# Interleaving two weight pieces by token tile, and moving one tile's norm from VectorE to ScalarE and GpSimd

## The chip, the core and the metric

The kernel runs on one NeuronCore of a Trainium2 chip. The metric is the device time of one execution in microseconds (us). The engines are TensorE (PE), VectorE (DVE), ScalarE (ACT), GpSimd (POOL) and SyncE (SP, which here only starts transfers). Each works through its own instruction stream in order and waits on semaphores for the others. All arithmetic is fp32; a product of two fp32 matrices is made of three matmuls on a high part (rounded to fp32r) and a low part (the rest) of each operand.

## The reference, cut to what matters

One decoder layer over 512 tokens of width 1024: a mixer of three attention-like parts, then cross attention into 256 memory tokens, then a mixture of experts, each with an RMS norm ahead and a residual add behind, and a final norm. The change lies between the second and the third:

```python
x = x + memory_cross_attention(rms_norm(x, xattn_norm_g), rms_norm(mem, mem_norm_g), wq, wk, wv, wo)
                                # its last step is  o @ wo,  512x1024 by 1024x1024
h = rms_norm(x, ffn_norm_g)     # x * rsqrt(mean(x*x) + EPS) * g, per token
coarse, fine = h @ w_coarse + b_coarse, h @ w_fine + b_fine     # 4 + 16 router logits a token
# group by argmax, top 2 of its 4 experts, then SwiGLU experts on the chosen tokens
```

## The kernel before, in words

The 512 tokens lie as four tiles of 128 (`NT` = 4), tile t in `X[:, t, :]`. Weights come in pieces of 128 x 2048 floats. For each piece SP loads it into one of three `raw` buffers, ACT copies it to a high part `whi`, DVE subtracts to a low part `wlo`, and PE multiplies. `whi` and `wlo` have two slots each (`SPLIT` = 2), so piece n is split only when piece n-2 has been multiplied to its end (`wait_consumed`).

The output projection `wo` of the cross attention is the last four pieces, `xo0` to `xo3` (`ND` is their end, so `xo2` is `ND - 2` and `xo3` is `ND - 1`). `xo0` and `xo1` are the upper and lower half of the contraction for output columns 0 to 511, `xo2` and `xo3` those for columns 512 to 1023. Each piece has four groups, one a token tile, of 12 matmuls 128x128 by 128x512. The groups of `xo2` and of `xo3` for a tile add into the same PSUM bank; DVE then adds the bank to X (the eviction, L1249). PE takes the pieces whole: all four tiles of `xo2`, then all four of `xo3`.

When a tile's last group is evicted, several engines work on that tile. Call this the tile's tail:

- ACT squares X with a row sum (`square_last`, L797); POOL makes the factor 1/rms from it (`rms`, L650 and L653, count `rms_done`); DVE writes h = X * factor * gain to `H3` in an interleaved column order (`norm_last`, L1165, count `h_done`). SP stores X to `xod` and H3 to `h3d`.
- PE transposes the unnormed X (`norm_transposes`, eight transposes to two banks, L1753); ACT copies them to `ahi` (`norm_hi`, L804), DVE subtracts to `alo` (`norm_lo`, L1172). The factor of a token is applied to its logits later, and the gain is already in the router weights.

Then PE multiplies the router weights with the tokens of tiles 0 and 1 into `ps[0]`, and with those of tiles 2 and 3 into `ps[1]` (`narrow`, 16 matmuls each, L1767 and L1769, count `route_mm`). ACT copies each out (`router_out`, L1025, to `rT`), PE turns them to token rows in `ps[2]` (`to_tokens`, L1774), and DVE starts a long chain of small instructions at L1467 that ends in the lists of tokens of each expert. Off that chain hang one-hot ranks on PE (L1944, L1948), the gather of the first expert's tokens by matmuls from H3 (L1956, which waits for `h_done`), the weight splits of the first expert's pieces (L791 on ACT, L1153 on DVE), and then the loop over the experts, six pieces a turn. After its splits ACT waits for `h_done` of all tiles, starts a transfer of the final gain, and makes two exponentials that DVE asks for at L1511.

In the kernel before, the transposes of tile 0 stand between the last two groups of `xo3`, those of tiles 1 to 3 after them. DVE runs `norm_last` of tiles 2 and 3 last, just ahead of L1467. SP asks for the expert pieces 6 to 9 only after `h_done` of all tiles.

Of the kernel before, what the change touches and what calls it, by code (L numbers as in the profile page):

```python
# [79 lines left out]
def build(nc, A, C, out):  # L80

    O = offsets()
    with ExitStack() as ctx:
# [3 lines left out]
        def sem(name):  # L87
            return ctx.enter_context(nc.semaphore(name))
# [196 lines left out]
            quarter(f"xo{b}", wo, b, NT, "dve")  # L285
        ND = len(pieces)
        NMP = ND + 4
        ORDER = sorted(KEY, key=KEY.get)
        of_piece = [[g for g, x in enumerate(groups) if x[0] == n] for n in range(ND)]

# [2 lines left out]
        sums = 0  # L293
        for g, x in enumerate(groups):
            if x[1] == "H" and x[3] == 1:
                tiles = len(of_piece[x[0]])
                bank_of.append(bank_of[g - tiles])
                before_bank.append(None)
            else:
                bank_of.append(sums % DRING)  # L300
                before_bank.append(last_on.get(sums % DRING))
                sums += 1
            if x[5]:
                last_on[bank_of[g]] = g
# [25 lines left out]
            return s2_hi[:, :], s2_lo[:, :]  # L330


        LATE_SPLITS = (KEY["win"], ND - 2, ND - 1)

        def evacs(g, eng):
# [94 lines left out]
        cum_mm = sem("cum_mm")  # L430
        cum_done = sem("cum_done")
        cumrow_in = sem("cumrow_in")
        kg_done = sem("kg_done")
        f_done = sem("f_done")
        fhi_done = sem("fhi_done")
        flo_done = sem("flo_done")
# [205 lines left out]
        def _(pool):  # L642
# [45 lines left out]
            pool.dma_start(Kf[64:65, :, :], C["ones"]).then_inc(rows_in, 16)  # L688
            for q in range(NT, N4):
                rms(q)  # L690

            pool.wait_ge(zero_out, 32)
            for t in range(NT):
# [66 lines left out]
        def _(act):  # L760
# [256 lines left out]
            def square_last(t):  # L1017

                act.wait_ge(evac["dve"], evacs(of_piece[ND - 1][t], "dve"))
                square(N3 + t, X[:, t, :], H3[:, t, :])  # L1020
# [4 lines left out]
                a.activation(rT[:, 2 * P * b:2 * P * (b + 1)], ps[b][0:2 * ROUT_W, 0:2 * P], ACT.Copy).then_inc(rT_done, 1)  # L1025

            act.wait_ge(PX.pv_done, len(UX))
            for t in range(3):
                square_last(t)
            for t in range(NT):  # L1030
                norm_hi(N3 + t, ahi, t)
            router_out(0)
            square_last(3)
            router_out(1)
            split_after(ND - 2)
            split_after(ND - 1)
            act.wait_ge(h_done, N4)
# [81 lines left out]
        def _(dve):  # L1119
# [326 lines left out]

                norm(N3 + t, X[:, t, :], H3[:, t, :])

            evacuate(ND - 1, (0, 1))
            norm_last(0)  # L1450
            evacuate(ND - 1, (2,))
            norm_last(1)
            norm_lo(N3, alo, ahi, 0)
            evacuate(ND - 1, (3,))
            for t in range(1, NT):
                norm_lo(N3 + t, alo, ahi, t)
            norm_last(2)
            norm_last(3)

            R = work[:, 0:2048]  # L1460

            def r3(at, c, t=NT):
                return R[:, at:at + t * c].rearrange("p (t c) -> p t c", t=t)

            L = r3(0, ROUT_W)
            dve.wait_ge(logits_done, 1)
            link(v.tensor_tensor(L, ps[2][:, 0:NT * ROUT_W].rearrange("p (t c) -> p t c", t=NT),  # L1467
                                 stat[:, 2, N3:N4].unsqueeze(2).to_broadcast([P, NT, ROUT_W]), ALU.mult))
            link(v.tensor_tensor(L, L, rbias[:, :].unsqueeze(1).to_broadcast([P, NT, ROUT_W]), ALU.add))
# [194 lines left out]
        def _(pe):  # L1664
# [23 lines left out]
                        ins = mm(bank[0:NB, 0:CMP_HID], x[:, 0:NB], lo[:, j, :], start=False, stop=False)  # L1688
                ins.then_inc(cw_used, 1)

            def dense(n):
                pe.wait_ge(lo_done, n + 1)
                hi = whi[:, n % SPLIT, :].rearrange("p (k n) -> p k n", k=KD)
                lo = wlo[:, n % SPLIT, :].rearrange("p (k n) -> p k n", k=KD)
                mem = ORDER[n][:2] in ("mk", "mv")
                xh, xl, nt = (memhi, memlo, MEM) if mem else (ahi, alo, T)
                for g in of_piece[n]:
                    _, kind, idx, c0, w, eng = groups[g]
                    if before_bank[g] is not None:
                        e = groups[before_bank[g]][5]  # L1700
                        pe.wait_ge(evac[e], evacs(before_bank[g], e))
                    bank = ps[bank_of[g]]
                    if ORDER[n] in ("out0", "xo0"):

                        pe.wait_ge((PA if ORDER[n] == "out0" else PX).ot_lo, 2 * (idx + 1))
                    if kind == "H":
                        tc = slice(idx * P, (idx + 1) * P)
                        h4, l4 = (x[:, n % SPLIT, :].rearrange("p (k n) -> p k n", k=KF) for x in (whi, wlo))
                        for k in range(KF):
                            kk = KF * c0 + k  # L1710
                            ins = three(bank[:, :], xh[:, kk, tc], xl[:, kk, tc], h4[:, k, :], l4[:, k, :],
                                        kk == 0, kk == KD - 1)
                        ins.then_inc(grp_done, 1)
                        if (ORDER[n], idx) == ("xo3", 2):
                            norm_transposes(N3, X[:, 0, :])
                        continue
                    for k in range(KD):
                        if kind == "F":
                            wc = slice(c0, c0 + P)
                            ins = three(bank[:, 0:nt], hi[:, k, wc], lo[:, k, wc], xh[:, k, :], xl[:, k, :],  # L1720
                                        k == 0, k == KD - 1)
                        else:
                            tc = slice(idx * P, (idx + 1) * P)
                            if n == 0 and k == 0:
                                pe.wait_ge(ntp_lo, 2 * (idx + 1))
                            if n == 0 and k == 3 and idx + 1 < NT:
                                norm_transposes(NX + idx + 1, tok[:, idx + 1, :])
                            ins = three(bank[:, 0:w], xh[:, k, tc], xl[:, k, tc], hi[:, k, c0:c0 + w],
                                        lo[:, k, c0:c0 + w], k == 0, k == KD - 1)
                    ins.then_inc(grp_done, 1)  # L1730
                    if (ORDER[n], idx) in part_after:
                        part(part_after[ORDER[n], idx])
                    if (ORDER[n], idx) == ("pool", 0):

                        pe.wait_ge(gelu_done, 2)
                        for m in range(4):
                            w = 2 * N_CMP
                            ins = nc.tensor.transpose(ps[6][:, w * m:w * (m + 1)],
                                                      gtok[:, m // 2, P * (m % 2):P * (m % 2 + 1)], ident[0:w, 0:w])
                        ins.then_inc(gT_mm, 1)  # L1740
# [183 lines left out]
                dense(n)  # L1924
            pe.wait_ge(evac["act"], evacs(of_piece[KEY["xo0"]][0] - 1, "act"))
            attention(PX)
            for n in range(KEY["xo0"], ND):
                dense(n)
            for t in range(1, NT):
                norm_transposes(N3 + t, X[:, t, :])  # L1930

            pe.wait_ge(sm_lo, 2)
            pe.wait_ge(evac["dve"], evacs(len(groups) - 1, "dve"))
            for b in range(2):
                pe.wait_ge(ntp_lo, 2 * (N3 + 2 * b + 2))
                narrow(ps[b], wrt2, ROUT_W, 2 * P * b, 2 * P).then_inc(route_mm, 1)
            pe.wait_ge(rT_done, 2)
            to_tokens(ps[2], rT, fold_r, ROUT_W).then_inc(logits_done, 1)

            pe.wait_ge(onehot_done, 1)  # L1940
# [161 lines left out]
```

## Time and profile before

| | |
|---|---|
| median of 3 runs | 837.52 us (837.29 to 839.09) |
| the profiled execution's own time | 837.84 us |
| its span, first to last instruction | 836.0 us |
| `xo0` to `xo3` on TensorE | from 448.8 us to 493.2 us |
| first instruction of the routing chain on VectorE (L1467) | 503.14 us |
| expert loop on TensorE | from about 533 us to about 810 us |

The rows show one execution; times in them count from the start of its span. The own time is 1.8 us above the span: what lies around the first and last instruction. A matmul's row begins when it starts and overlaps the next one; a full 128x512 matmul follows the one before it 0.23 us later.

### The profile page before, as it was taken

To read this page: it belongs to the slowest core of one execution; us is meant where nothing else is said; L and a number is where in the kernel's file an instruction comes from. 1 tells how busy PE (TensorE), PEld (TensorE's weight loads), DVE (VectorE), ACT (ScalarE), POOL (GpSimd) and SP (SyncE) were. 2 spreads that over 40 slices of the span, in tenths; PEclk is the share of its full clock that TensorE was granted. 3 is DMA by queue.
4 is the path that set the end of the run, shared out by engine and by line. 5 is a ranking of instruction groups with operands and counts; after the bars stand their busy time and mean duration, and the time that the engine had idled before them with its cause. 6 is when DMAs were issued, how large, how long until landed. Compare 5 with 4: busy or idle time off the path is not lost.

```text
span 836.0 us, 11923 instructions
## 1 busy us (share of the span) xinstructions
PE 775.4 (93%) x4188; PEld 615.9 (74%) x4188; DVE 522.6 (63%) x753; ACT 462.7 (55%) x673; POOL 183.0 (22%) x175
## 2 busy tenths in 40 slices
PE   3999999999999999999899995999999999999960
PEld 3978789887778889888687875677777777777740
DVE  4454356576554445532353369988899898998942
ACT  4465532576565215632342143677778887778742
POOL 2910000000000102000000010224456544565222
PEclk9999999999999999999999996999999999999995
DMA  9825430000041533652200467799999999999916
GB/s 284 225 79 152 137 117 1 1 2 2 2 152 52 176 126 112 196 171 100 101 1 1 180 252 303 285 397 377 379 386 390 372 382 369 387 388 373 371 22 220
DMA packets 61776, 167.63 MB, mean 201 GB/s; under 512 B 7942, under 2 KB 35910, under 8 KB 49446
## 3 DMA queue, kind: packets, MB, share of 16 engines
q1 hardware_dynamic: 56376, 150.69, 48.5%
q0 software_dynamic: 4352, 13.20, 6.9%
q10 hardware_dynamic: 1008, 3.21, 1.1%
q8 instruction: 25, 0.41, 0.2%
q14 instruction: 15, 0.12, 0.0%
HBM read 153.42 MB, written 13.63 MB: 200 GB/s over the span
## 4 chain that ended last, share of the span: by engine, by line
PE 53%; DMA 17%; POOL 11%; DVE 7%; issue 7%; ACT 3%; POOLq 1%; SPq 0%; ACTq 0%; DVEq 0%
DMA xod<-tok,yidx 16%; PE ps L1669 11%; PE ps L1671 11%; PE ps L1670 11%; POOL yidx L699 7%; PE ps L1894 6%; PE ps L1851 5%; PE ps L1868 3%; PE ps L1846 2%; PE ps L1753 1%; DVE wlo L1145 1%; POOL tok L710 1%; POOL spare L707 1%; ACT whi L778 1%; DVE wlo L1153 1%
## 5 line engine op out<-in xcount | busy, mean ns | idle before, releaser
L1145 DVE TENSOR_TENSOR wlo<-raw,whi 128x2048 fp32r<-128x2048 f32 x30 | 68.7, 2291 | 113.8 <-ACT whi L778 113.8
L1669 PE MATMUL ps<-whi,mhi 128*96 128x512 f32 (+1 forms) x288 | 114.2, 397 | 2.7 <-DVE mlo L1627 1.2
L650 POOL TENSOR_SCALAR stat<-stat 128x1 f32<-128x1 f32 x18 | 13.6, 758 | 462.8 <-ACT tok L797 304.8
L1671 PE MATMUL ps<-whi,mlo 128*96 128x512 f32 (+1 forms) x288 | 113.6, 394 | 0.0
L1670 PE MATMUL ps<-wlo,mhi 128*96 128x512 f32 (+1 forms) x288 | 112.9, 392 | 0.0
L1153 DVE TENSOR_TENSOR wlo<-arena,whi 128x2048 fp32r<-128x2048 f32 x40 | 91.5, 2291 | 14.9 <-ACT whi L791 14.8
L791 ACT ACTIVATE whi<-arena 128x2048 fp32r<-128x2048 f32 x40 | 76.7, 1917 | 28.8 <-PE ps L1671 28.8
L778 ACT ACTIVATE whi<-raw 128x2048 fp32r<-128x2048 f32 x30 | 57.3, 1910 | 63.4 <-PE ps L1671 63.3
L1669 PE MATMUL ps<-ahi,whi 128*128 128x512 f32 x192 | 75.8, 395 | 0.0
L1670 PE MATMUL ps<-alo,whi 128*128 128x512 f32 x192 | 75.3, 392 | 0.0
L1671 PE MATMUL ps<-ahi,wlo 128*128 128x512 f32 x192 | 75.2, 391 | 0.0
L1669 PE MATMUL ps<-whi,ahi 128*128 128x512 f32 (+1 forms) x192 | 69.3, 361 | 4.8 <-DVE wlo L1145 4.8
L1671 PE MATMUL ps<-whi,alo 128*128 128x512 f32 (+1 forms) x192 | 68.3, 356 | 0.0
L1670 PE MATMUL ps<-wlo,ahi 128*128 128x512 f32 (+1 forms) x192 | 68.3, 356 | 0.0
L1669 PEld LDWEIGHTS ps<-whi,mhi 128*96 128x96 f32 (+1 forms) x288 | 47.3, 164 | 21.1 <-issue 2.4
L1671 PEld LDWEIGHTS ps<-whi,mlo 128*96 128x96 f32 (+1 forms) x288 | 47.3, 164 | 19.2
L1670 PEld LDWEIGHTS ps<-wlo,mhi 128*96 128x96 f32 (+1 forms) x288 | 47.4, 165 | 18.2
L699 POOL TENSOR_TENSOR yidx<-ltok,zeroi 96x1 int32<-96x1 int32 x16 | 58.9, 3682 | 0.3
L1374 DVE TENSOR_REDUCE nmax<-ps 128x1 f32<-128x256 f32 (+3 forms) x88 | 41.8, 477 | 24.6 <-PE ps L1852 17.8
L965 ACT ACTIVATE work<-ps,nmax 128x256 f32<-128x256 f32 (+3 forms) x66 | 34.0, 515 | 37.3 <-DVE nmax L1374 36.7
L1851 PE MATMUL ps<-arena 128*128 128x128 f32 (+3 forms) x144 | 53.8, 456 | 0.9 <-ACT work L965 0.9
L1669 PE MATMUL ps<-s_hi,mhi 128*96 128x512 f32 x128 | 51.2, 400 | 0.0
(316 smaller groups left out, 1708.5 us busy)
## 6 DMA issues: line engine op xcount, KB each, us to landing
arena<-in_exp_w_gate SPq DMA_DIRECT2D x30, 1024.0 KB
arena<-in_exp_w_up SPq DMA_DIRECT2D x17, 1024.0 KB
raw_a<-in_exp_w_down SPq DMA_DIRECT2D x16, 1024.0 KB, 19.2
raw<-in_exp_w_up SPq DMA_DIRECT2D x15, 1024.0 KB, 16.6
arena<-in_exp_w_down SPq DMA_DIRECT2D x9, 1024.0 KB
raw<-in_exp_w_down SPq DMA_DIRECT2D x7, 1024.0 KB, 17.8
raw<-in_w_in SPq DMA_DIRECT2D x5, 1024.0 KB, 5.7
raw<-in_w_in SPq DMA_DIRECT2D x10, 512.0 KB, 8.7
```

The lines of the kernel that those rows point to most:

```text
L699: pool.tensor_tensor(dst[0:CHUNK, :], ltok[0:CHUNK, bass.ds(c, 1)], zeroi[0:CHUNK, :], ALU.add).then_inc(steps, 1)
L778: a.activation(whi[:, n % SPLIT, :], raw[:, n % RAW, :], ACT.Copy).then_inc(hi_done, 1)
L791: a.activation(moe_split(m)[0], moe_raw(m), ACT.Copy).then_inc(hi_done, 1)
L965: a.activation(Pr[s % len(Pr)][:, 0:nk], ps[s % 3][:, 0:nk], ACT.Exp, bias=nmax[:, c:c + 1], accum_out=den[:, c:c + 1]).then_inc(ph.exp_do ...
L1145: v.tensor_tensor(wlo[:, n % SPLIT, :], raw[:, n % RAW, :], whi[:, n % SPLIT, :].bitcast(F32), ALU.subtract).then_inc(lo_done, 1)
L1153: v.tensor_tensor(lo, moe_raw(m), hi.bitcast(F32), ALU.subtract).then_inc(lo_done, 1)
L1374: v.tensor_reduce(nmax[:, c:c + 1], ps[s % 3][:, 0:nk], AX.X, ALU.max, negate=True)\
L1669: mm(out_, ahi_, bhi_, start=first, stop=False)
L1670: mm(out_, ahi_, blo_, start=False, stop=False)
L1671: return mm(out_, alo_, bhi_, start=False, stop=last)
L1851: mm(bank[:, 0:P * nb], q, kk, start=True, stop=False)
L1894: ins = mm(bank[:, 0:w], pt[:, P * b:P * (b + 1)], val, start=(b == 0), stop=(b == nb - 1))
```

## The change

The groups of the last two pieces are reordered: for each token tile, its `xo2` group, then its `xo3` group. The PSUM banks stay one a tile. The transposes of tile t-1 come right after the `xo3` group of tile t, those of tile 3 after everything, and the two router products follow. On ACT the squares and the high copies interleave in a new order. The fourth tile's norm leaves DVE: ACT multiplies X by the factor into H3, and POOL multiplies that by the gain in place.

```diff
+        tail = groups[-2 * NT:]
+        groups[-2 * NT:] = [tail[NT * b + t] for t in range(NT) for b in range(2)]
...
-                tiles = len(of_piece[x[0]])
+                tiles = 1 if x[0] == ND - 1 else len(of_piece[x[0]])
...
@@ gpsimd, after the loop over rms(q)
+            pool.wait_ge(gain_full, 64)
+            pool.wait_ge(h_done, N4 - 1)
+            pool.wait_ge(last_scaled, 1)
+            h_last = H3[:, 3, :].rearrange("t (k q) -> t q k", k=KD)
+            pool.tensor_tensor(h_last, h_last, gbc[:, :].rearrange("t (q k) -> t q k", k=KD), ALU.mult).then_inc(h_done, 1)
@@ scalar
-            for t in range(3):
-                square_last(t)
-            for t in range(NT):
-                norm_hi(N3 + t, ahi, t)
+            square_last(0)
+            square_last(1)
+            norm_hi(N3, ahi, 0)
+            square_last(2)
+            norm_hi(N3 + 1, ahi, 1)
+            norm_hi(N3 + 2, ahi, 2)
             router_out(0)
+            norm_hi(N3 + 3, ahi, 3)
             square_last(3)
             router_out(1)
+            act.wait_ge(rms_done, N4)
+            a.activation(H3[:, 3, :].rearrange("t (k q) -> t q k", k=KD), X[:, 3, :].rearrange("t (q k) -> t q k", k=KD),
+                         ACT.Copy, scale=stat[:, 2, N4 - 1:N4]).then_inc(last_scaled, 1)
             split_after(ND - 2)
             split_after(ND - 1)
             act.wait_ge(h_done, N4)
@@ vector
-            evacuate(ND - 1, (0, 1))
-            norm_last(0)
-            evacuate(ND - 1, (2,))
-            norm_last(1)
-            norm_lo(N3, alo, ahi, 0)
-            evacuate(ND - 1, (3,))
-            for t in range(1, NT):
-                norm_lo(N3 + t, alo, ahi, t)
-            norm_last(2)
-            norm_last(3)
+            for t in range(NT):
+                evacuate(ND - 1, (t,))
+                if t:
+                    norm_lo(N3 + t - 1, alo, ahi, t - 1)
+                if t < 3:
+                    norm_last(t)
+            norm_lo(N3 + 3, alo, ahi, 3)
...
             dve.wait_ge(logits_done, 1)
+            dve.wait_ge(rms_done, N4)
@@ tensor
-                        if (ORDER[n], idx) == ("xo3", 2):
-                            norm_transposes(N3, X[:, 0, :])
...
-            for n in range(KEY["xo0"], ND):
-                dense(n)
-            for t in range(1, NT):
-                norm_transposes(N3 + t, X[:, t, :])
-
-            pe.wait_ge(sm_lo, 2)
-            pe.wait_ge(evac["dve"], evacs(len(groups) - 1, "dve"))
-            for b in range(2):
+            dense(KEY["xo0"])
+            dense(KEY["xo1"])
+            for t in range(NT):
+                dense(ND - 2, (t,))
+                dense(ND - 1, (t,))
+                if t:
+                    norm_transposes(N3 + t - 1, X[:, t - 1, :])
+
+            def router(b):
+                pe.wait_ge(sm_lo, 2)
+                pe.wait_ge(evac["dve"], evacs(of_piece[ND - 1][b], "dve"))
                 pe.wait_ge(ntp_lo, 2 * (N3 + 2 * b + 2))
                 narrow(ps[b], wrt2, ROUT_W, 2 * P * b, 2 * P).then_inc(route_mm, 1)
+
+            norm_transposes(N3 + 3, X[:, 3, :])
+            router(0)
+            router(1)
             pe.wait_ge(rT_done, 2)
+            pe.wait_ge(evac["dve"], evacs(of_piece[ND - 1][2], "dve"))
             to_tokens(ps[2], rT, fold_r, ROUT_W).then_inc(logits_done, 1)
```

`dense` on PE takes the token tiles to multiply as an argument; each call still waits for the low part of its piece (`lo_done`).

## Rows read from the trace of the kernel before

**Rows 1.** Busy time by stretch, the expert loop: us, busy (x matmuls), granted clock, DMA share, GB/s.

```profile
700.00:750.00 50.00, 50.00 (x239) 1.00 1.02 377
```

**Rows 2.** TensorE in order of time: start us, us, line, operation, tiles, [idle <- releaser].

```profile
473.30 0.39 PE L1669 MATMUL ps<-whi,ahi 128*128 128x512 f32 x1
...
493.00 0.39 PE L1671 MATMUL ps<-whi,alo 128*128 128x512 f32 x1
...
495.94 1.06 PE L1753 MATMUL ps<-ident,arena 128*128 128x128 f32 x8 [0.79 <-DVE alo L1172]
496.75 0.36 PE L1767 MATMUL ps<-ahi,wrt 128*40 128x256 f32 x1
...
498.60 0.40 PE L1767 MATMUL ps<-ahi,wrt 128*40 128x256 f32 x2
...
501.22 1.07 PE L1774 MATMUL ps<-fold_r,work 40*128 40x20 f32 x8 [0.47 <-ACT work L1025]
...
511.23 9.90 PE L1956 MATMUL ps<-work,arena 128*128 128x96 f32 x64 [2.19 <-DVE work L1527]
```

**Rows 3.** The chain that ended last, the early transposes: start us, us, piece.

```profile
489.79 0.88 PE ps L1753 x8
```

**Rows 4.** VectorE in order of time.

```profile
472.79 2.29 DVE L1145 TENSOR_TENSOR wlo<-raw,whi 128x2048 fp32r<-128x2048 f32 x1 [1.32 <-ACT whi L778]
...
493.58 0.68 DVE L1249 TENSOR_TENSOR arena<-ps,arena 128x512 f32<-128x512 f32 x1
...
501.27 2.02 DVE L1165 SCALAR_TENSOR_TENSOR arena<-arena,stat,gbc 128x1024 f32<-128x1024 f32 x1 [0.75 <-POOL stat L653]
503.14 0.22 DVE L1467 TENSOR_TENSOR work<-ps,stat 128x80 f32<-128x80 f32 x1
...
508.37 0.16 DVE L1511 TENSOR_REDUCE work<-work 128x4 f32<-128x16 f32 x1
...
521.99 1.01 DVE L1584 TENSOR_TENSOR mlo<-ps,mhi 128x384 fp32r<-128x384 f32 x2
```

**Rows 5.** ScalarE in order of time.

```profile
493.87 2.06 ACT L804 ACTIVATE ahi<-ps 128x512 fp32r<-128x512 f32 x4 [1.20 <-PE ps L1753]
...
498.91 0.38 ACT L1025 ACTIVATE work<-ps 40x256 f32<-40x256 f32 x1 [1.23 <-PE ps L1767]
...
500.79 0.38 ACT L1025 ACTIVATE work<-ps 40x256 f32<-40x256 f32 x1 [0.46 <-PE ps L1767]
501.07 3.70 ACT L791 ACTIVATE whi<-raw 128x2048 fp32r<-128x2048 f32 x2
...
537.92 1.91 ACT L791 ACTIVATE whi<-arena 128x2048 fp32r<-128x2048 f32 x1
```

**Rows 6.** TensorE's busy time and granted clock in single microseconds (columns as in Rows 1).

```profile
412.00:413.00 1.00, 0.00 (x0) 1.00 0.00 0
414.00:415.00 1.00, 1.00 (x5) 0.59 0.85 295
447.00:448.00 1.00, 0.13 (x1) 1.00 0.00 0
503.00:504.00 1.00, 0.00 (x0) 0.50 0.96 373
513.00:514.00 1.00, 1.00 (x7) 0.50 1.01 426
518.00:519.00 1.00, 1.00 (x12) 1.00 0.04 16
```

**Rows 7.** Groups by line, GpSimd: names, shapes, count | busy us, mean ns | idle.

```profile
L681 POOL MEMSET arena<- 64x11264 f32 x1 | 9.5, 9522 | 0.0
```

**Rows 8.** Groups by line and shape, VectorE.

```profile
L1165 DVE SCALAR_TENSOR_TENSOR tok<-arena,stat,gbc 128x1024 f32<-128x1024 f32 x12 | 15.4, 1282 | 25.2 <-POOL stat L653 25.2
...
L1165 DVE SCALAR_TENSOR_TENSOR arena<-arena,stat,gbc 128x1024 f32<-128x1024 f32 x4 | 8.3, 2079 | 0.7 <-POOL stat L653 0.7
```

**Rows 9.** SyncE's queue in order of time.

```profile
505.21 0.86 SPq L575 DMA_DIRECT2D arena<-in_exp_w_up  x2
```

More of the change, by code:

```diff
@@ L330, in moe_split @@
             return s2_hi[:, :], s2_lo[:, :]
+        LOGIT_BANKS = [bank_of[of_piece[ND - 1][t]] for t in range(NT)]
+        assert LOGIT_BANKS == list(range(NT))
         LATE_SPLITS = (KEY["win"], ND - 2, ND - 1)
@@ L432, in build @@
         cumrow_in = sem("cumrow_in")
-        kg_done = sem("kg_done")
+        last_scaled = sem("last_scaled")
         f_done = sem("f_done")
@@ L1689, in part, with dense @@
                 ins.then_inc(cw_used, 1)
-            def dense(n):
+            def dense(n, only=range(NT)):
                 pe.wait_ge(lo_done, n + 1)
@@ L1698, in dense @@
                     _, kind, idx, c0, w, eng = groups[g]
+                    if idx not in only:
+                        continue
                     if before_bank[g] is not None:
```

## The prediction

> **What bounds the kernel now.** I read first the busy times by stretch, for the expert loop: TensorE is busy for 50.00 of 50.00 us [rows 1]. From the loop's first turn to its last TensorE waits for nothing, so a turn has a fixed length, and whatever moves the loop's start moves the end of the kernel by the same amount. The transfers run at a share of 1.02 there, but a loop short of weights would show idle TensorE.
>
> What sets the loop's start? I followed the chain backward and then the timelines engine by engine. From 503.14 us, the first instruction of the routing chain, to 523 us VectorE runs its small instructions nearly back to back [rows 4]; the one piece beside it that is about as long is the gather, 9.90 us on TensorE from 511.23 us, over at 521.13 us [rows 2], against the low part that follows it on VectorE at 521.99 us [rows 4]. So the question is when VectorE can start L1467. In the kernel before the logits were there at 501.22 + 1.07 = 502.29 us [rows 2], and VectorE came 0.85 us later, because the fourth tile's norm held it until 503.29 us; the two overlap by their pipeline [rows 4].
>
> **Part 1: the order of the groups.** The matmuls stay the same in number. But the first group of `xo3` now comes after one group of `xo2`, at 473.30 us, where before the second group of `xo2` stood [rows 2]. `xo3` can be split only when `xo1` has been multiplied, as before, and its low part is written at 472.79 + 2.29 = 475.08 us [rows 4]. Before, three more groups of `xo2` covered that. TensorE therefore stands for 475.08 - 473.30 = 1.8 us, with 0.1 for starting again: 1.9 us. Then the transposes of two tiles, not of one, lie ahead of the last group: +0.9 us [rows 3]. The last matmul of the projection starts at 493.00 + 1.9 + 0.9 = 495.8 us [rows 2].
>
> What this buys is that tiles 0 to 2 are norm-ready early. Per tile the new spacing is 5.4 us and more, two groups of 12 matmuls at 0.23 us, while VectorE has 0.7 us of eviction, 1.3 us of low part and 2.1 us of norm a tile: all of that is hidden, and VectorE is free for the last eviction.
>
> **Part 2: the fourth tile's tail.** Its eviction ended 0.58 + 0.68 = 1.26 us after the start of the last matmul (493.58 + 0.68 = 494.26 us) [rows 2, 4]. After the change: 495.8 + 1.3 + 0.1 = 497.2 us for the start of the transposes of tile 3, against 495.94 us. The first router product starts 0.81 us after them, as before: 498.0 us instead of 496.75 us [rows 2].
>
> Now ACT. Its new order has `router_out(0)` ahead of the high copy of tile 3. ACT works in order, and `router_out(0)` waits for the first router product, which stands on TensorE behind the transposes of tile 3. So the high copy, ready to run at 497.9 us, is queued behind a wait that ends 498.91 - 496.75 = 2.16 us after the product's start [rows 2, 5], at 500.1 us. With 0.28 us between two such starts (500.79 and 501.07 us) the high copy starts at 500.4 us. From the start of a high copy to the next use of the low part by TensorE took 495.94 - 493.87 = 2.07 us [rows 2, 5], so the second router product starts at 502.5 us, where before it followed the first at 498.72 us, the second of the pair at 498.60 us [rows 2]. That is +3.8 us. TensorE has nothing else in its queue: it idles from about 499.9 us.
>
> From there the steps are those of before: `router_out(1)` 500.79 - 498.72 = 2.07 us later, the token rows 0.43 us after it, and 1.07 us of them [rows 2, 5]. 502.5 + 2.07 + 0.43 + 1.07 = 506.1 us. VectorE no longer has `norm_last(3)` in front (its last work is the low part of tile 3), so L1467 starts at once, at about 506.15 us instead of 503.14 us: the removed norm of 2.02 us gives back only the 0.85 us that it was late. **Sum so far: +3.0 us** (the work moved +3.8, the norm -0.8).
>
> **Part 3: the clock.** TensorE ran at a granted clock of 1.00, that is 2.4 GHz, until its small products ended, and at 0.50, 1.2 GHz, in the microsecond from 503 us [rows 6]. An idle microsecond at 412 us, in a gap of about 2.2 us, was followed by a fall at 414 us; the gap of about 1.5 us at 447 us was not [rows 6]. The new gap before the second router product is about 2.5 us, longer than both, and around it stand the same narrow products and small waits after which the clock fell in the kernel before. I take it to fall before or in the second router product. Price: 16 products took 498.60 - 496.75 = 1.85 us; at half clock they take double, as the gather's rows do (7 starts a us at 0.50, 12 at 1.00) [rows 6], and so do the 1.07 us of token rows. Bounds 0 and 2.9 us. I take 1.6 us, a fall in the middle of the product.
> The Trainium skill ("TensorE: Matmul & The Clock Gate", Part 1) says that the throttled state is the default, that activity releases it, and that the moment varies from run to run; the trace agrees as far as rows 6 show both levels and returns to the full one only in work. By that rule the sum is 4.6 us where the fall comes in the product, 3.0 us where it comes later.
>
> **Part 4: the norm on ACT and POOL.** Relative to the start L of L1467, `router_out(1)` starts at L - 1.6; the scaling on ACT follows at L - 1.3. No row has it; the nearest are ACT's copies of 128x512, 2.06 us for four [rows 5], so about 1.1 us for 1024 columns, and VectorE's own norm takes 2079 ns with the interleaved write, 1282 ns without [rows 8], a ratio of 1.62. I take 1.4 us: done at L + 0.1. POOL's multiply isn't in the trace either. The only wide row of POOL writes 11264 elements in 9522 ns, 0.85 ns each [rows 7]: 0.87 us for 1024 is the lower bound. Two reads and a write one after the other are 2.6 us, times 1.62 for the interleaved order 4.2 us, which I take; double that, 8.4 us, if it shares its accesses with VectorE, is the upper bound. Who waits: SP's loads of pieces 6 to 9, at 505.21 us before [rows 9]; they slip to about 511 us, but ACT first takes piece 6 at 537.92 us [rows 5], which itself moves later. The gather starts 8.1 us after L. ACT's splits (3.70 us for two [rows 5]) end at L + 3.8, then it stands at `h_done` until L + 4.3, starts a transfer (0.43 us for one, half of two [rows 9]) and makes two short exponentials: L + 5.1. VectorE asks for them at 508.37 - 503.14 = 5.2 us after L [rows 4]. So 4.2 us is just covered: price 0. Each us beyond 4.3 moves the end by one.
> The Trainium skill ("GPSIMD Engine Reference", 3.1 and 7) has GpSimd about twice as slow as VectorE on a two-input fp32 operation and half as slow again for wide strides; by it an estimate for this multiply is 3.8 us. No run here shows it yet, and it would leave the sum as it is.
>
> **Sum.** 3.0 + 1.6 + 0 = +4.6 us, all of it ahead of a chain that passes it on. The profiled execution's own time of 837.84 us becomes 842.4 us, its span 836.0 us becomes 840.6 us. The profiled execution is 0.3 us above the median, so the predicted median is 837.52 + 4.6 = 842.1 us.
>
> **Rivals.**
> - **A, the clock holds** through the second router product. For: it held over the gap at 447 us. Against: that one lay among wide matmuls. Time 837.5 + 3.0 = 840.5 us.
> - **B, POOL is late.** If its multiply takes more than 4.3 us, ACT's exponentials reach L1511 late. For: nothing like it was run, ACT and VectorE both show a cost for the interleaved order, and VectorE reads two tensors all the time beside it. At 6.3 us it adds 2 us, at 8.4 us 4 us: 844 to 846 us. The same skill page (8, Key points) says that GpSimd shares its access to SBUF with VectorE instructions of two SBUF inputs; the chain's instructions are largely of that kind. By the rule either side gets longer, and this rival weighs more; no run here shows it yet.
> - **C, the clock falls at the first stall too**, at 473 to 475 us, 1.9 us idle. The wide matmuls then run at half clock for some 3 us, as at 414 us, and lose 1.5 us: 843.6 us. Against: it is wide work before and behind.
> - **D, not slower.** The hold on ACT costs nothing: it decides if `router_out(0)` can start before 497.9 us, 2.2 us earlier than I have it. Then the second product follows the first at 499.9 us, and L1467 starts at 503.5 us: +0.4 us, 837.9 us; without the first stall as well, 836.0 us. Against: both are plain order on one engine.
>
> **Numbers.** Chances: forecast 0.45 (its own range 841.2 to 843.2 us), A 0.25, B 0.15, C 0.07, D 0.08. About 0.2%, 1.7 us, is what a measurement of this kernel can tell from no change. Faster 0.03 and same 0.05 are D's; all others are slower, 0.92. The range 839.6 to 844.8 us holds forecast, A and C and the lower part of B, and leaves out D and the end of B.
>
> **What would show it.** TensorE idle for about 1.8 us before the first matmul of `xo3`, released by VectorE's L1145; the last projection matmul near 495.8 us; the high copy of tile 3 on ACT directly behind `router_out(0)`; 2.5 us of idle TensorE between the two router products; the granted clock at 0.50 in the second; L1467 near 506 us at full clock, 507.7 us with the fall; POOL's multiply near 4 us and L1511 not waiting. Wrong would be: the second product following at once, a projection without the stall, L1467 before 505 us, or a loop in which TensorE waits and so absorbs the shift.

## The result, and the profile after

The changed kernel takes 844.42 us (median of six runs, 842.25 to 848.28), the kernel before 838.23 us (six runs). The ratio is 1.0073, 95% interval 1.0048 to 1.0097. Timed again in the session of some of the experiments it is 1.0080 (1.0067 to 1.0093). So it is slower by 6 to 7 us; the forecast was 4.6 us.

The profiled execution of the changed kernel is the slowest of its six: 848.28 us, span 846.4 us, against 836.0 us before. Not all of these 10.4 us are the change. The first matmul of the output projection, TensorE in order of time, already comes 3.0 us later than in the kernel before (448.69 us), ahead of everything that was edited:

```profile
451.67 0.48 PE L1682 MATMUL ps<-whi,ahi 128*128 128x512 f32 x1
```

All comparisons below therefore count from that matmul, called P. The routing chain's first instruction (then L1467, now L1480) was at P + 54.45 us before; the low part of the gathered tokens, the first product of the chain that TensorE waits for, came 18.85 us later. These two stretches hold the whole change: from that low part to the end of the span it takes 314.0 us before and 314.2 us in the changed kernel.

VectorE of the changed kernel in order of time (start us, us, line, operation, [idle <- releaser]), the counterpart of [rows 4]:

```profile
475.75 2.29 DVE L1160 TENSOR_TENSOR wlo<-raw,whi 128x2048 fp32r<-128x2048 f32 x1 [1.32 <-ACT whi L787]
...
503.94 1.29 DVE L1187 TENSOR_TENSOR alo<-ps,ahi 128x512 fp32r<-128x512 f32 x2 [2.30 <-ACT ahi L813]
510.82 0.24 DVE L1480 TENSOR_TENSOR work<-ps,stat 128x80 f32<-128x80 f32 x1 [5.59 <-PE ps L1787]
511.10 0.24 DVE L1482 TENSOR_TENSOR work<-work,rbias 128x80 f32<-128x80 f32 x1
511.37 0.17 DVE L1485 TENSOR_REDUCE work<-work 128x4 f32<-128x16 f32 x1
511.58 2.63 DVE L1487 TENSOR_TENSOR work<-work 128x16 f32<-128x16 f32 x1
514.13 0.16 DVE L1492 TENSOR_TENSOR work<-work 128x16 f32<-128x16 f32 x1
...
532.15 1.01 DVE L1597 TENSOR_TENSOR mlo<-ps,mhi 128x384 fp32r<-128x384 f32 x2
```

The chain starts at 510.82 - 451.67 = P + 59.15 us, 4.70 us later than before, and VectorE idles 5.59 us ahead of it, waiting for TensorE. Then one instruction of 128x16 (L1487) takes 2.63 us; the next one of its kind and size, L1492, takes 0.16 us. The low part of the gathered tokens comes 532.15 - 510.82 = 21.33 us behind the chain's start, 2.48 us more than before. 4.70 + 2.48 = 7.2 us; with the 3.0 us ahead of P that is the span's 10.4 us but for 0.2.

TensorE in order of time, the counterpart of [rows 2]; the first row is the first matmul of `xo3`:

```profile
478.10 0.50 PE L1682 MATMUL ps<-whi,ahi 128*128 128x512 f32 x1 [1.67 <-DVE wlo L1160]
...
499.10 2.04 PE L1766 MATMUL ps<-ident,arena 128*128 128x128 f32 x16
500.89 0.36 PE L1780 MATMUL ps<-ahi,wrt 128*40 128x256 f32 x1
...
502.74 0.27 PE L1780 MATMUL ps<-ahi,wrt 128*40 128x256 f32 x1
...
505.38 0.28 PE L1780 MATMUL ps<-ahi,wrt 128*40 128x256 f32 x1 [2.36 <-DVE alo L1187]
...
508.89 1.89 PE L1787 MATMUL ps<-fold_r,work 40*128 40x20 f32 x8 [0.47 <-ACT work L1034]
```

ScalarE in order of time, the counterpart of [rows 5]:

```profile
499.73 1.09 ACT L813 ACTIVATE ahi<-ps 128x512 fp32r<-128x512 f32 x2 [3.95 <-PE ps L1766]
503.05 0.38 ACT L1034 ACTIVATE work<-ps 40x256 f32<-40x256 f32 x1 [2.24 <-PE ps L1780]
503.33 1.06 ACT L813 ACTIVATE ahi<-ps 128x512 fp32r<-128x512 f32 x2
...
508.46 0.38 ACT L1034 ACTIVATE work<-ps 40x256 f32<-40x256 f32 x1 [3.03 <-PE ps L1780]
508.75 2.02 ACT L1048 ACTIVATE arena<-arena,stat 128x1024 f32<-128x1024 f32 x1
...
514.62 0.22 ACT L1057 ACTIVATE work<-work 128x16 f32<-128x16 f32 x1 [0.35 <-DVE work L1487]
517.99 0.20 ACT L1059 ACTIVATE work<-work 128x4 f32<-128x4 f32 x1 [3.15 <-DVE work L1513]
```

The first router copy at 503.05 us, and the high copy of tile 3 directly behind it at 503.33 us; the second product at 505.38 us, after 2.36 us of idle TensorE. GpSimd in order of time:

```profile
511.32 2.87 POOL L699 TENSOR_TENSOR arena<-arena,gbc 128x1024 f32<-128x1024 f32 x1 [4.98 <-ACT arena L1048]
```

POOL's multiply runs from 511.32 to 514.19 us. VectorE's long instruction begins at 511.58 us and is over at 514.21 us, with it. The granted clock (columns as in [rows 1], busy and clock of TensorE):

```profile
504.00:505.00 1.00, 0.00 (x0) 1.00 0.00 0
505.00:506.00 1.00, 0.62 (x6) 1.00 0.00 0
506.00:507.00 1.00, 1.00 (x8) 0.53 0.00 0
507.00:508.00 1.00, 1.00 (x6) 0.50 0.00 0
```

### The profile page after: what moved, and what is told of

It is laid out like the page before. It is cut to its first block, busy times and chain, and to the rows that moved or that the text cites. A ratio compares the mean times of both kernels' runs of the same rounds, so it can differ in the third digit from the quotient of the medians.

```text
span 846.4 us, 11931 instructions
## 1 busy us (share of the span) xinstructions
PE 780.5 (92%) x4188; PEld 619.8 (73%) x4188; DVE 523.7 (62%) x752; ACT 464.7 (55%) x674; POOL 186.0 (22%) x176
## 4 chain that ended last, share of the span: by engine, by line
PE 56%; DMA 17%; POOL 10%; DVE 6%; issue 6%; ACT 2%; POOLq 1%; SPq 0%; ACTq 0%; DVEq 0%
DMA xod<-tok,yidx 16%; PE ps L1682 12%; PE ps L1684 12%; PE ps L1683 12%; POOL yidx L708 7%; PE ps L1907 6%; PE ps L1864 5%; PE ps L1881 3%; PE ps L1766 2%; PE ps L1859 2%; POOL tok L719 1%; DVE wlo L1160 1%; POOL spare L716 1%; ACT whi L787 1%; PE ps L1834 1%
## 5 line engine op out<-in xcount | busy, mean ns | idle before, releaser
L1684 PEld LDWEIGHTS ps<-whi,mlo 128*96 128x96 f32 (+1 forms) x288 | 47.3, 164 | 19.2
L711 POOL TENSOR_TENSOR yw<-lwt,spare 96x1 f32<-96x1 f32 x16 | 27.1, 1694 | 110.0 <-DMA xod<-tok,yidx 110.0
```

Of the source, the lines that this page charges most:

```text
L1684: return mm(out_, alo_, bhi_, start=False, stop=last)
```

## The experiments

Each ran on the chip against the kernel before in the same session. The ratios are over all executions of a kernel, the two trace columns (in us) from one profiled execution each.

| kernel | chain starts at P + | from there to the gathered tokens' low part | ratio to the kernel before (95%) |
|---|---|---|---|
| before | 54.45 | 18.85 | 1 |
| changed | 59.15 | 21.33 | 1.0073 (1.0048 to 1.0097) |
| changed, again | 59.20 | 21.32 | 1.0080 (1.0067 to 1.0093) |
| e1, norm on VectorE | 59.02 | 18.86 | 1.0061 (1.0041 to 1.0082) |
| e2, high copy first | 54.92 | 21.52 | 1.0046 (1.0031 to 1.0062) |
| e3, gap filled | 57.29 | 21.45 | 1.0085 (1.0067 to 1.0103) |
| e4, POOL with one input | 58.57 | 20.49 | 1.0077 (1.0057 to 1.0096) |
| e5, covered split | 58.65 | 21.44 | 1.0062 (1.0047 to 1.0077) |
| e6 = e1 + e2, square of tile 3 earlier | 54.90 | 18.89 | 1.0006 (0.9993 to 1.0020) |
| b1 = e5 + e6 | 54.59 | 18.87 | 1.0007 (0.9996 to 1.0018) |
| e7, scaling early | 58.78 | 19.86 | 1.0068 (1.0054 to 1.0083) |
| e8, the norm's part alone | 53.61 | 21.46 | 1.0015 (1.0007 to 1.0024) |
| b2 = b1, norm of tile 2 later | 53.63 | 18.86 | 0.9983 (0.9975 to 0.9992) |

Outside of these columns the traces differ in one place. From the low part of the gathered tokens to the end of the span all thirteen take 313.9 to 314.4 us. But P lies between 451.2 and 451.7 us in three of them (changed, changed again, e2) and between 447.5 and 448.8 us in the other ten, though no edit touches what comes before it. So two times can differ by 3 us for reasons that have nothing to do with the edits, and why P moves is not shown. The ratios move less than the trace columns: the columns of e2 add up to 4.0 us less than those of the changed kernel, the ratios differ by 2.3 to 2.8 us. I take sizes from the trace columns and directions from both.

**The changed kernel again.**

> The changed kernel unaltered, as the yardstick for the three others on the same chip: 1.0055 to 1.0095 of the kernel before by its first timing, some 6 us slower. In the profile the routing chain should again start about 59 us after the first matmul of the output projection (54.45 us in the kernel before), and one two-input instruction of VectorE should again stand for about 2.5 us while POOL multiplies.

Both numbers returned to within 0.05 us, so the two delays are not the chance of one execution.

**e1, the fourth tile's norm on VectorE.**

```diff
-            pool.tensor_tensor(h_last, h_last, gbc[:, :].rearrange("t (q k) -> t q k", k=KD), ALU.mult).then_inc(h_done, 1)
...
-            a.activation(H3[:, 3, :].rearrange("t (k q) -> t q k", k=KD), X[:, 3, :].rearrange("t (q k) -> t q k", k=KD),
-                         ACT.Copy, scale=stat[:, 2, N4 - 1:N4]).then_inc(last_scaled, 1)
...
             norm_lo(N3 + 3, alo, ahi, 3)
+            norm_last(3)
```

> Edit: the fourth tile's norm is back on VectorE, behind its last low part and ahead of the routing chain; ACT's scaling and POOL's multiply are gone. The rest is the changed kernel. Theory S (shared access): the 2.63 us of one routing instruction that takes 0.17 us before (2.46 us more) is VectorE with two SBUF inputs standing still while POOL's 2.87 us multiply runs. Without it every routing instruction is as short as before, and VectorE does the norm in the 5.6 us in which it idles ahead of the chain: the time falls by 2.5 us against the changed kernel, to about 842 us. Rival theory W (a wait elsewhere): the long instruction comes from something else at that moment, such as ACT's splits or a semaphore; then it stays long and the time falls by at most 0.3 us. Rival theory N: the norm costs VectorE its 2.1 us again, and nothing is gained.

VectorE, ahead of the chain and in it:

```profile
503.41 2.02 DVE L1172 SCALAR_TENSOR_TENSOR arena<-arena,stat,gbc 128x1024 f32<-128x1024 f32 x1 [1.14 <-POOL stat L657]
507.72 0.24 DVE L1473 TENSOR_TENSOR work<-ps,stat 128x80 f32<-128x80 f32 x1 [2.30 <-PE ps L1780]
...
508.48 0.17 DVE L1480 TENSOR_TENSOR work<-work 128x16 f32<-128x16 f32 x1
```

The norm runs in VectorE's idle time, and the long instruction is gone: 18.86 us, as before. Theory S holds in the trace at its full 2.5 us; theories W and N fall. The timing moved less, from 1.0073 or 1.0080 to 1.0061, and the intervals overlap, so by the clock alone this run would not settle it.

**e2, the high copy first.**

```diff
-            router_out(0)
             norm_hi(N3 + 3, ahi, 3)
+            router_out(0)
```

> Edit: on ACT the high copy of tile 3 stands ahead of the copy of the first router product; nothing else. Theory H (hold): the second router product waited 2.4 us for a high copy that was ready but queued behind the first product. It then follows the first at once, TensorE has no gap there, and the granted clock stays at 1.00 through product and token rows, which gives back 1.0 + 0.8 us more: about 4.2 us faster than the changed kernel in the profile, 2.4 us if the clock falls nevertheless. POOL's multiply still stops VectorE for some 2.5 us. Rival: the low part on VectorE is what comes late, not the high copy; then the gap stays and under 0.5 us is gained.

The chain starts 4.2 us earlier, as theory H says, and TensorE has no wait between the products. The time fell as well, 1.0046. It tells the hold and the clock's price together (59.15 to 54.92 us), not each by itself; the rival is out.

**e3, the gap filled.**

```diff
             router(0)
+            pe.wait_ge(evac["dve"], evacs(of_piece[ND - 1][3], "dve"))
+            narrow(ps[3], wrt2, ROUT_W, 0, 2 * P)
             router(1)
```

> Edit: 16 more narrow matmuls of the first router product, into a bank that nobody reads, stand between the two router products, in the 2.4 us in which TensorE idles. They take 1.9 us. Nothing is left out. Theory C (clock): the fall of the granted clock to 0.50 in the second product comes from that gap; filled, it stays at 1.00, the product takes 1.9 us again and the token rows 1.07 us: 1.8 us faster than the changed kernel. Rival: the clock falls for narrow work as well, since it fell right after such work in the kernel before; then no gain, and at half clock the filler itself makes the product later by up to 1.4 us.

In the trace the clock stays at 1.00 until 508 us, past the token rows at 504.15 us, and the chain starts 1.9 us earlier. The microsecond of the token rows (columns as in [rows 1]):

```profile
504.00:505.00 1.00, 0.85 (x8) 1.00 0.00 0
```

The timing, though, does not show it: 1.0085, no better than the changed kernel. The profiled execution was the fastest of its six (842.49 us, the slowest 846.08 us), so it may not stand for the others. I leave the discrepancy open.

What the traces as a set do show: in all six with the gap of 2.36 us before the second product (changed, changed again, e1, e4, e5, e7) the granted clock falls to 0.50 ahead of or in that product; in all seven without it (before, e2, e3, e6, e8, b1, b2) it stays at 1.00 until the token rows end. The price is 0.9 to 1.5 us in the product (2.96 to 3.60 us from its start to the second copy, 2.07 us before), and 0.8 us in the token rows where it lasts (changed kernel, again, e1). In e4, e5 and e7 the clock was back for the token rows, 1.1 us, as e7's rows show (us, busy, clock):

```profile
503.00:504.00 1.00, 1.00 (x6) 0.50 0.00 0
504.00:505.00 1.00, 1.00 (x7) 0.50 0.00 0
505.00:506.00 1.00, 0.53 (x5) 1.00 0.00 0
506.00:507.00 1.00, 0.76 (x7) 1.00 0.02 8
```

**e4, POOL with one input.**

```diff
-            pool.tensor_tensor(h_last, h_last, gbc[:, :].rearrange("t (q k) -> t q k", k=KD), ALU.mult).then_inc(h_done, 1)
+            pool.tensor_scalar(h_last, h_last, 1.0, None, ALU.mult).then_inc(h_done, 1)
```

> Edit: POOL multiplies the fourth tile by 1.0 in place, one SBUF input, in place of the multiply by the gain with two. It leaves out the gain of the fourth tile in the rows that the experts gather. Theory S in its narrow form (two inputs on both sides): a POOL instruction with one input does not stop VectorE; all routing instructions stay at 0.17 us and the time falls by 2.5 us. Theory S in its wide form: any POOL instruction that reads SBUF stops VectorE's two-input instructions while it runs; one of them is longer by what is left of POOL's instruction when it comes, less than 2.5 us if the one-input form is shorter. Theory W: the long instruction stays at 2.6 us whatever POOL's instruction takes.

POOL, ScalarE that waits for it, and VectorE beside it:

```profile
508.23 4.57 POOL L699 TENSOR_SCALAR arena<-arena 128x1024 f32<-128x1024 f32 x1 [5.19 <-ACT arena L1048]
```

```profile
513.24 0.22 ACT L1057 ACTIVATE work<-work 128x16 f32<-128x16 f32 x1 [2.08 <-POOL arena L699]
```

```profile
508.21 0.17 DVE L1494 TENSOR_REDUCE work<-work 128x4 f32<-128x16 f32 x1
508.42 1.79 DVE L1495 TENSOR_TENSOR work<-work 128x16 f32<-128x16 f32 x1
510.25 0.23 DVE L1501 TENSOR_TENSOR work<-work 128x64 f32<-128x64 f32 x1
...
511.01 0.17 DVE L1492 TENSOR_TENSOR work<-work 128x16 f32<-128x16 f32 x1
```

Neither form of theory S fits whole. Beside a POOL instruction with one input VectorE's instruction does stand (1.79 us in place of 0.17 us), so the narrow form falls. But it ran for 4.57 us, longer than the multiply with two inputs, and held VectorE for 1.6 us only: from 510.25 us on, instructions with two inputs ran at their usual 0.17 to 0.23 us beside it. ACT waited for POOL until then (2.08 us ahead of its first exponential), so POOL's length is real. Why VectorE was let go midway is open.

**e5, the covered split.**

```diff
-        groups[-2 * NT:] = [tail[NT * b + t] for t in range(NT) for b in range(2)]
+        groups[-2 * NT:] = [tail[i] for i in (0, 1, 4, 2, 5, 3, 6, 7)]
-                tiles = 1 if x[0] == ND - 1 else len(of_piece[x[0]])
-                bank_of.append(bank_of[g - tiles])
+                bank_of.append(bank_of[of_piece[x[0] - 1][x[2]]])
...
+            dense(ND - 2, (0,))
             for t in range(NT):
-                dense(ND - 2, (t,))
+                if t < 3:
+                    dense(ND - 2, (t + 1,))
                 dense(ND - 1, (t,))
```

> Edit: the eight groups of the last two pieces in the order xo2 tile 0, xo2 tile 1, xo3 tile 0, xo2 tile 2, xo3 tile 1, xo2 tile 3, xo3 tile 2, xo3 tile 3; the rest as in the changed kernel. Theory L (late low part): the 1.8 us stall of TensorE is the second split, not yet written after one group; with two groups of 2.7 us ahead it is. The routing chain starts 1.9 us earlier against the projection's first matmul (57.2 us instead of 59.1) and the time falls by 1.9 us. Rival: the stall comes from PSUM or from the alternation of two pieces, and stays in some form; then nothing is gained.

Who TensorE waited for, in total us, times and the longest, between 440 and 545 us, first in the changed kernel, then in e5:

```profile
PE ps L1780 <- DVE alo L1187: 2.4, 1, 2.4
...
PE ps L1682 <- DVE wlo L1160: 1.7, 1, 1.7
```

```profile
PE ps L1779 <- DVE alo L1186: 2.4, 1, 2.4
...
PE ps L1765 <- DVE arena L1263: 1.7, 1, 1.7
```

The wait for the split is gone, and the last projection matmul starts at P + 45.20 us instead of P + 47.20: theory L is right about the stall. But the chain gained 0.5 us only, and of these 0.2 us by the start of the second router product (P + 53.52 against 53.71 us); the rest is the clock, which was back for the token rows. A new wait stands in its place: the transposes of tile 3 (L1765) wait for its eviction, because VectorE was in the norm of tile 2:

```profile
493.51 1.99 DVE L1179 SCALAR_TENSOR_TENSOR arena<-arena,stat,gbc 128x1024 f32<-128x1024 f32 x1
495.35 0.68 DVE L1263 TENSOR_TENSOR arena<-ps,arena 128x512 f32<-128x512 f32 x1
```

**e6 and b1, the three together, without and with the covered split.** The edits are those above, and on ACT `square_last(3)` ahead of both router copies.

> Edit: the group order of the changed kernel, but the fourth tile's norm back on VectorE (behind its last low part), and on ACT the high copy and the square of tile 3 ahead of both copies of router products. If hold, clock and shared access are separate and add up, this is 4.2 + 2.5 = 6.7 us faster in the profile than the changed kernel: the chain starts about 55 us after the projection's first matmul and takes the 18.85 us of the kernel before until the low part of the gathered tokens. Time 0.5 us above the kernel before. If one of the three covers another, it stays 2 us or more above.

> Edit: all of e5 and e6 together: covered split, high copy and square of tile 3 first, norm on VectorE. What the interleaving was able to give: the last projection matmul 0.9 us later than in the kernel before, but the transposes of tile 3 need not wait for a bank (0.79 us before), and the norm of tile 3 is done before the logits come. The routing chain starts about 53.1 us after the projection's first matmul, 1.3 us earlier than in the kernel before: 836.5 us against 837.8 us, a ratio of 0.9985. Rival: VectorE's norm of tile 3 still ends after the logits, and the time is that of the kernel before.

e6 came out as added up: P + 54.90 and 18.89 us, ratio 1.0006. So what e1 and what e2 give back add up: the shared access is one price, the hold with the clock another. e6 does not part the hold from the clock; that rests on e3's trace. b1 came out otherwise than I expected: it meets the same new wait as e5, 1.7 us at the transposes of tile 3, and gains 0.3 us on e6 in the trace and nothing in the time. The rival that I had named (the norm of tile 3) was not the reason; it was the norm of tile 2.

**e7, the scaling early.**

```diff
             square_last(3)
-            router_out(1)
             act.wait_ge(rms_done, N4)
             a.activation(H3[:, 3, :].rearrange("t (k q) -> t q k", k=KD), X[:, 3, :].rearrange("t (q k) -> t q k", k=KD),
                          ACT.Copy, scale=stat[:, 2, N4 - 1:N4]).then_inc(last_scaled, 1)
+            router_out(1)
```

> Edit: in the changed kernel ACT scales the fourth tile ahead of the second router copy, not behind it, while it waits for that product anyway; POOL's multiply therefore runs some 3 us earlier, before the routing chain starts. The same instructions on the same engines. Theory S (VectorE's instruction with two SBUF inputs stands while POOL's multiply runs, so only the overlap costs): the routing chain starts as in the changed kernel, 59.2 us after the projection's first matmul, and from its start to the low part of the gathered tokens it takes 18.9 to 19.2 us, not 21.3: 2.2 us faster. Rival: the cost comes from having POOL's instruction or ACT's scaling at all; then the 21.3 us stay.

POOL, then VectorE:

```profile
505.34 2.85 POOL L699 TENSOR_TENSOR arena<-arena,gbc 128x1024 f32<-128x1024 f32 x1 [2.67 <-ACT arena L1047]
```

```profile
506.80 0.24 DVE L1480 TENSOR_TENSOR work<-ps,stat 128x80 f32<-128x80 f32 x1 [5.24 <-PE ps L1787]
507.08 1.22 DVE L1482 TENSOR_TENSOR work<-work,rbias 128x80 f32<-128x80 f32 x1
508.33 0.17 DVE L1485 TENSOR_REDUCE work<-work 128x4 f32<-128x16 f32 x1
```

The same instructions cost 1.0 us instead of 2.5 us (19.86 us, expected 18.9 to 19.2: the chain came earlier against POOL than I reckoned). The instruction held is another one now, L1482, the first with two SBUF inputs that comes while POOL runs, and it ends where POOL's ends, at 508.2 to 508.3 us. What costs is the overlap. The ratio, 1.0068, moved by 0.4 to 1.0 us only, and the intervals overlap: the trace carries this reading. The first instruction, L1480, reads one input from PSUM and is not held.

**e8, the norm's part alone in the kernel before.** The edit of POOL, ACT and `norm_last(3)` as in the changed kernel; the order of groups, transposes and ACT's copies is that of before. VectorE waits for `rms_done` ahead of the chain, as in the changed kernel.

> Edit: the kernel before with one part of the change alone: the fourth tile's norm on ACT and POOL, no interleaving, ACT's order as before. The norm no longer holds VectorE ahead of the chain: the chain starts 0.75 us earlier (53.7 us after the projection's first matmul, 54.45 before). POOL's multiply then falls into the chain: 21.4 us instead of 18.85 us by theory S. Net 1.8 us slower than the kernel before, 839.7 us. Rival: without the interleaving the multiply is hidden, and the part alone is 0.75 us faster.

P + 53.61 and 21.46 us: 0.84 us gained, 2.61 us lost, 1.8 us in sum; timed 1.0015 (1.0007 to 1.0024), 1.3 us. This part alone makes the kernel slower. POOL took 2.86 us from 503.79 us; VectorE's instruction in that stretch ends with it, at 506.72 us:

```profile
503.92 2.80 DVE L1496 TENSOR_TENSOR work<-work 128x64 f32<-128x64 f32 x1
```

**b2, the norm of tile 2 behind the low part of tile 3.**

```diff
-                if t < 3:
+                if t < 2:
                     norm_last(t)
             norm_lo(N3 + 3, alo, ahi, 3)
+            norm_last(2)
             norm_last(3)
```

> Edit: as the version with covered split, high copy first and norm on VectorE, which lost what the covered split gave because VectorE was in the norm of tile 2 when tile 3's eviction came (TensorE waited 1.7 us there); here the norm of tile 2 stands behind the low part of tile 3. The transposes of tile 3 start 1.6 us earlier, and the routing chain starts 53.0 to 53.4 us after the projection's first matmul, 1.0 to 1.4 us earlier than in the kernel before; some 0.3 us of that depend on the two norms being over when the logits come. Time 836.7 us where the kernel before has 837.9 us. Rival: the two norms behind each other hold the chain as the one did in the kernel before, and nothing is gained.

```profile
493.28 0.69 DVE L1255 TENSOR_TENSOR arena<-ps,arena 128x512 f32<-128x512 f32 x1
...
496.74 2.07 DVE L1171 SCALAR_TENSOR_TENSOR arena<-arena,stat,gbc 128x1024 f32<-128x1024 f32 x1
499.40 2.03 DVE L1171 SCALAR_TENSOR_TENSOR arena<-arena,stat,gbc 128x1024 f32<-128x1024 f32 x1 [0.59 <-POOL stat L656]
501.26 0.23 DVE L1473 TENSOR_TENSOR work<-ps,stat 128x80 f32<-128x80 f32 x1
```

TensorE no longer waits for an eviction, and the chain starts at P + 53.63 us, 0.8 us earlier than before; the kernel is a little faster than the one before: 836.22 against 837.97 us, ratio 0.9983 (0.9975 to 0.9992). The token rows were there at about 500.5 us (they start at 499.45 us and take 1.07 us), so the norm of tile 3 still holds the chain for 0.7 us: the rest of what I expected.

That norm started late because it waited 0.59 us for the factor from POOL, and POOL's first instruction for it, which took 0.19 us for each of the tiles before, took 1.81 us. It ended at 498.73 us, with VectorE's norm of tile 2 (496.74 to 498.81 us):

```profile
496.92 1.81 POOL L653 TENSOR_SCALAR stat<-stat 128x1 f32<-128x1 f32 x1 [4.48 <-ACT arena L800]
```

So here POOL stood while a VectorE instruction with two SBUF inputs ran. The trace of the kernel before shows the same: its 18 instructions of this kind (L650) take 0.19 to 1.29 us. The 13 of them that take 0.28 us or more all start while a VectorE instruction with two SBUF inputs runs (L1145 or L1165) and end within 0.1 us of its end; four of the other five start beside none, and the fifth starts 0.1 us before the end of one. One such pair, over at 489.79 and 489.73 us:

```profile
487.70 2.09 DVE L1165 SCALAR_TENSOR_TENSOR arena<-arena,stat,gbc 128x1024 f32<-128x1024 f32 x1
```

```profile
489.06 0.67 POOL L650 TENSOR_SCALAR stat<-stat 128x1 f32<-128x1 f32 x1 [1.77 <-ACT arena L797]
```

No experiment isolates this direction.

## Why the prediction was right, and where it failed

The direction, the place and the range (839.6 to 844.8 us) were right. That the time fell into the range is in part luck. It lies above the forecast's own range (841.2 to 843.2 us) and 0.4 us below the upper end, which stood that high for rivals C and B; neither happened, and their room covered a price that the sum did not have. Against that, the kernel before took 838.23 us over six executions and 837.52 us over the three that the forecast started from, 0.7 us that no step forecast. By its own steps, against P:

- Part 1, stall and transposes: predicted 2.8 us for the last projection matmul, measured 2.9 us (P + 47.20 against P + 44.31). e5 shows that the stall is the late split.
- Part 2, the hold on ACT: predicted +3.8 us for the second router product, measured 505.38 - 451.67 = 53.7 against 50.0 us, +3.7. e2 shows that ACT's order alone makes it.
- Part 3, the clock: predicted 1.6 us, measured 1.0 us until the second copy (508.46 - 505.38 = 3.08 us instead of 2.07) and 0.8 us in the token rows, 1.8 us. That the gap brings it rests on the thirteen traces, six against seven; the timing of e3 does not show it. The 1.6 us were called a fall in the middle of the product, but by the prediction's own terms that is 0.9 + 1.07 = 2.0 us. The sum for the chain's start, 4.6 us, met 4.7.
- Part 4 is the step that failed. Its sizes were off in both directions: 2.02 us instead of 1.4 for the scaling, 2.87 us instead of 4.2 for POOL's multiply. (Its own rows give 1.1 x 1.62 = 1.8 us for the scaling; and the rows of before that it names show a cost of the interleaved order for VectorE only, not for ACT, as rival B has it.) The exponentials came in time, as predicted (at 517.99 us ACT had waited 3.15 us for VectorE, and not for POOL, which ended at 514.19 us). But "price 0" was wrong: the multiply costs 2.5 us through VectorE's instructions with two inputs from SBUF, which stand while it runs: e1 shows it by taking the multiply away, e7 by moving it. Rival B had the time (844 to 846 us) and the shared access, but as a longer POOL instruction that makes ACT late; what happened is the other side of it, a short POOL instruction and a VectorE that stands, at a place where nothing waits for POOL. Even in e4, where POOL was done only 5.85 us after the chain's start, beyond B's limit of 4.3 us, VectorE never waited for the exponentials, since the hold had moved VectorE later too.
- Rival A did not occur in any of the six traces with the gap, C in none of the eight with the first stall. D, that the hold on ACT costs nothing, fell with e2.

By the trace the change costs 7.2 us, by the two ratios 6.1 and 6.7 us. The interval of the second timing, 5.6 to 7.8 us, holds both.

What would have named it was in sight. The trace of the kernel before has 13 small POOL instructions that were held beside VectorE's instructions with two SBUF inputs (see b2); the prediction did not read them, and said that no run showed shared access yet. And the Trainium skill ("GPSIMD Engine Reference", 8, Key points) says that GpSimd shares its SBUF interfaces with VectorE, with contention where VectorE's instruction has two SBUF inputs. The trace agrees: 2.46 us on an instruction with two inputs, nothing on L1485, a reduction with one input at 511.37 us beside the running POOL, which kept its 0.17 us. The prediction gave it a rival, but no term in the sum.

## What to carry to other kernels

When two pieces of work are interleaved, look first at what the second one needs: here its split was covered by the three groups that were moved away, and an order with two groups ahead keeps the cover. A wait placed ahead of a ready instruction on an in-order engine costs as long as the ready work is held, here 2.4 us, and the gap that it made on TensorE cost 1.8 us of clock on top. Work moved to GpSimd "off the path" was not free here, because VectorE had instructions with two SBUF inputs to do in that time: 2.5 us for an overlap of 2.6 us, 1.0 us for one of 1.1 us. So put such work where VectorE idles, or leave it on VectorE, and look the other way round as well: small POOL instructions stood beside VectorE's, up to 1.81 us in b2.

## What was not expected of the hardware

- A POOL multiply of 128x1024 with two inputs, one of them and the output in an interleaved order, took 2.85 to 2.87 us in seven traces; a multiply by a constant with one input, in the same order, took 4.57 us in the one trace that has it.
- Beside the two-input form, the VectorE instruction with two SBUF inputs that came first ended with POOL's instruction in all seven traces, at most 0.11 us after it (1.22 us in e7, 2.63 to 2.85 us in the others, in place of 0.17 to 0.24 us). They were four different instructions of the chain. Beside the one-input form it was held for 1.6 us, and its followers ran at full speed while POOL's still ran.
- The other way round, POOL's instruction of 128x1 took up to 1.29 us in the kernel before and 1.81 us in b2, in place of 0.19 us, where a VectorE instruction with two SBUF inputs was running, and ended within 0.1 us of its end.
- ACT's scaling of 128x1024 into the interleaved order took 2.02 us, the square of the same size in plain order 1.05 us.
